# First mixer norm: squares summed along the token rows as loaded, factors spread by TensorE, no barrier, transposes at once

## The reference, cut to what matters

```
def rmsnorm(x, g):
    xf = x.astype(jnp.float32)
    y = xf * lax.rsqrt(jnp.mean(xf * xf, axis=-1, keepdims=True) + EPS)
    return (y * g.astype(jnp.float32)).astype(x.dtype)
...
xn = rmsnorm(x, norm_mix[l])
...
q, f, i, g = jnp.split(xn @ w_in, 4, axis=-1)
```

## Time and profile before

| | |
|---|---|
| median of 3 runs | 2931.27 us (2928.22 to 2931.78) |
| the profiled execution | 2926.66 us, of which the span of its instructions is 2924.9 us |
| mean granted TensorE clock | 0.978 of 2.4 GHz |
| busy share of the span | PE 95%, DVE 42%, ACT 20%, POOL 37% |
| chain of work that ended last | PE 87%, DVE 7%, ACT 2% |

### The profile page before, as it was taken

How to read it: one execution, slowest core, us unless ns; L and a number is a source line. 1 busy time by engine, 2 the same in 40 slices (tenths; PEclk the granted TensorE clock), 3 DMA queues, 4 the chain that set the end, 5 groups by cost and what they waited for, 6 DMA issues and landing times.

```text
span 2924.9 us, 43391 instructions
## 1 busy us (share of the span) xinstructions
PE 2790.2 (95%) x17613; PEld 2698.3 (92%) x17613; DVE 1240.5 (42%) x2145; ACT 580.5 (20%) x1158; POOL 1080.4 (37%) x938
## 2 busy tenths in 40 slices
PE   4999999989999999999999999976999999999998
PEld 3999999979999999999999887765799999999998
DVE  6244445443533333333361444556543333333335
ACT  4122222221300000000020233345030000000003
POOL 4333333313444334433346313311443443344331
PEclk7999999989999999999999999988999999999999
DMA  3111111131111111111122111145321111111211
GB/s 102 37 45 52 52 52 52 50 105 45 44 44 44 58 44 44 44 53 49 44 89 65 58 40 48 53 139 188 112 58 44 44 45 57 44 44 44 58 44 59
DMA packets 202239, 175.04 MB, mean 60 GB/s; under 512 B 6290, under 2 KB 185093, under 8 KB 202062
## 3 DMA queue, kind: packets, MB, share of 16 engines
q1 hardware_dynamic: 161728, 138.49, 15.3%
q10 hardware_dynamic: 40334, 33.95, 3.6%
HBM read 147.06 MB, written 25.36 MB: 59 GB/s over the span
## 4 chain that ended last, share of the span: by engine, by line
PE 87%; DVE 7%; ACT 2%; DMA 1%; POOL 1%; issue 1%; SPq 0%; ACTq 0%; PEld 0%; DVEq 0%; POOLq 0%; PEldq 0%
PE ps L709 25%; PE ps L711 25%; PE ps L710 25%; PE ps L904 3%; PE ps L1128 2%; PE ps L1148 1%; DMA k_page<-in_cache_k 1%; DVE rstd L1857 1%; DVE k_page L2196 1%; DVE stats L2130 1%; ACT probs L1621 1%; DVE act_lo L1862 1%; DVE act_whole L1814 1%; PE ps L1236 0%; PE ps L937 0%
## 5 line engine op out<-in xcount | busy, mean ns | idle before, releaser
L709 PE MATMUL ps<-act_hi,w_hi 128*128 128x344 f32 (+2 forms) x3808 | 1244.1, 327 | 30.2 <-DVE act_lo L1840 15.0
L711 PE MATMUL ps<-act_hi,w_lo 128*128 128x344 f32 (+2 forms) x3808 | 1221.4, 321 | 0.0
L710 PE MATMUL ps<-act_lo,w_hi 128*128 128x344 f32 (+2 forms) x3808 | 1221.4, 321 | 0.0
L668 POOL TENSOR_TENSOR w_hi<-w_stage,ones 128x512 fp32r<-128x512 f32 (+1 forms) x412 | 429.1, 1072 | 1382.8 <-PEq L759 1306.7
L709 PEld LDWEIGHTS ps<-act_hi,w_hi 128*128 128x128 f32 x3808 | 719.4, 189 | 46.9 <-issue 32.5
L710 PEld LDWEIGHTS ps<-act_lo,w_hi 128*128 128x128 f32 x3808 | 719.4, 189 | 3.8 <-issue 2.0
L711 PEld LDWEIGHTS ps<-act_hi,w_lo 128*128 128x128 f32 x3808 | 719.1, 189 | 0.0
L672 POOL TENSOR_TENSOR w_lo<-w_stage,w_hi 128x512 fp32r<-128x512 f32 (+1 forms) x412 | 540.0, 1342 | 8.1
L2044 DVE TENSOR_TENSOR resid<-resid,ps 128x344 f32<-128x344 f32 x528 | 269.9, 513 | 188.8 <-PE ps L711 188.5
L709 PE MATMUL ps<-h_hi,w_hi 128*128 128x344 f32 x1056 | 339.2, 321 | 2.6 <-DVE resid L2044 2.6
L710 PE MATMUL ps<-h_lo,w_hi 128*128 128x344 f32 x1056 | 337.1, 319 | 0.0
(11 more groups left out here) (279 smaller groups left out, 2225.3 us busy)
## 6 DMA issues: line engine op xcount, KB each, us to landing
w_stage<-in_w_gate_up SPq DMA_DIRECT2D x88, 512.0 KB, 4.9
w_stage<-in_w_down SPq DMA_DIRECT2D x44, 512.0 KB, 3.9
w_stage<-in_w_in_a SPq DMA_DIRECT2D x32, 512.0 KB, 5.2
w_stage<-in_w_kv SPq DMA_DIRECT2D x16, 512.0 KB, 4.3
k_page<-in_cache_k SPq DMA_DIRECT2D x16, 512.0 KB, 4.4
v_page<-in_cache_v SPq DMA_DIRECT2D x16, 512.0 KB, 6.3
w_stage<-in_w_out_b SPq DMA_DIRECT2D x12, 512.0 KB, 4.6
x_spill<-resid ACTq DMA_DIRECT2D x8, 516.0 KB, 2.9
```

The costliest lines, as they stand in the source:

```text
L668: last = g.tensor_tensor(hi[:, part], WST[:, part], ones[:, 0:1].to_broadcast([P, quarter]), ALU.mult)
L709: pe.matmul(out, wh, xh, start=first, stop=False)
L710: pe.matmul(out, wh, xl, start=False, stop=False)
L711: return pe.matmul(out, wl, xh, start=False, stop=last)
```

## The change

The factors no longer come from the transposed stream. ACT squares each block as it lies in `xs`, tokens on partitions, with an accumulated sum per row into a column of `frs` (`final_rstd`), then takes Ln and Exp of those 8 columns (and of one for the sample rows). DVE multiplies the identity by each column: eight 128x128 diagonal matrices and one of 8x8, in chunk 7 of `act_whole`. TensorE multiplies them by a matrix of ones, which spreads each token's factor over all partitions, into PSUM banks 6 and 7 (and 4 for the sample columns). DVE's product of X, gain and factor reads those banks in place of `rstd`, over 1024 columns; the 8 sample columns are done apart.

The transposes use three pairs of banks in turn and begin once the identity, the ones and the epsilon column stand (`consts` 1; the masks behind them raise it to 2, which PE, ACT and DVE wait for later). DVE alone copies a whole block of `X`. The barrier is gone. POOL's split of slab 1 waits until all 8 rests of the first norm are made, and ACT waits for the lower-bound vectors (`lb_ready`) ahead of its first evacuation. The small-vector work of DVE moves: its first part behind the copies of `X`, its second behind the last rest.

```diff
-        def phases_through(name):
-            return 3 * (PHASES.index(name) + 1)
-
-        def barrier(eng, name):
-
-            eng.drain().then_inc(phase_done, 1)
-            eng.wait_ge(phase_done, phases_through(name))
-
...
@@ GpSimd @@
+            g.memset(epst[:], EPS).then_inc(consts, 1)
             step(g.memset(pick[:], 0.0))
             step(g.memset(pick[:, 7:8], 1.0))
-            step(g.memset(epst[:], EPS))
...
+                if n == 1:
+                    pool.wait_ge(operand_split, C)
...
@@ TensorE @@
-            def norm(ph, squares):
-
-                pe.wait_ge(norm_acc, (nth(ph) + 1) * (C - 1))
-                for t in range(NT):
-                    last = pe.matmul(PS[:, t, 0:TS], ones[:], squares[:, 0, tile(t)], start=True, stop=True)
-                last.then_inc(norm_ss_full, 1)
-
...
             pe.wait_ge(consts, 1)
+            for b in range(NB):
+                pe.wait_ge(chunk_in[b], 16)
+                if b > 2:
+                    pe.wait_ge(io_copied[0], b - 2)
+                for c in range(C):
+                    last = pe.transpose(PS[:, 2 * (b % 3) + c // 4, c % 4 * P:(c % 4 + 1) * P], xs[:, b, c * P:(c + 1) * P], ident[:])
+                last.then_inc(io_full[0], 1)
             pe.wait_ge(vec_in, 16 * 11)
             pe.transpose(PS[:, 7, 0:78], RS[0:78, 0:P], ident[0:78, 0:78]).then_inc(vec_full, 1)
+            pe.wait_ge(xs_in, 16)
+            pe.wait_ge(io_copied[0], 6)
+            for c in range(C):
+                last = pe.transpose(PS[:, 4, c * DEC:(c + 1) * DEC], xss[:, c * P:(c + 1) * P], ident[0:DEC, 0:DEC])
+            last.then_inc(io_full[0], 1)
+            pe.wait_ge(vec_ready, 1)
+            pe.matmul(PS[:, 5, 0:2], ones[:], lam[:, 6:8], start=True, stop=True).then_inc(lam_full, 1)
             for b in range(NB):
-                pe.wait_ge(chunk_in[b], 16)
-                for u in range(2):
-                    q = 2 * b + u
-                    if b:
-                        pe.wait_ge(io_copied[u], b)
-                    for c in range(4):
-                        last = pe.transpose(PS[:, q % 2, c * P:(c + 1) * P], xs[:, b, (4 * u + c) * P:(4 * u + c + 1) * P], ident[:])
-                    last.then_inc(io_full[u], 1)
-            pe.wait_ge(xs_in, 16)
-            pe.wait_ge(io_copied[0], NB)
-            for c in range(C):
-                last = pe.transpose(PS[:, 0, c * DEC:(c + 1) * DEC], xss[:, c * P:(c + 1) * P], ident[0:DEC, 0:DEC])
-            last.then_inc(io_full[0], 1)
-
-            pe.wait_ge(vec_ready, 1)
-            pe.matmul(PS[:, 6, 0:2], ones[:], lam[:, 6:8], start=True, stop=True).then_inc(lam_full, 1)
-            barrier(pe, "loaded")
-            norm("mix0", XL32)
+                pe.wait_ge(x_diag, b + 1)
+                pe.matmul(PS[:, 6 + b // 4, b % 4 * P:(b % 4 + 1) * P], ones[:], XL32[:, C - 1, b * P:(b + 1) * P],
+                          start=True, stop=True)
+            pe.wait_ge(x_diag, NB + 1)
+            pe.matmul(PS[:, 4, 0:DEC], ones[0:DEC, :], XL32[0:DEC, C - 1, SEQ:T], start=True, stop=True).then_inc(norm_ss_full, 1)
+            pe.wait_ge(consts, 2)
...
@@ ScalarE @@
-            def square_block(b):
-
-                act.wait_ge(io_copied[0], b + 1 + (b == NB - 1))
-                act.wait_ge(io_copied[1], b + 1)
-                a.activation(XH32[:, :, block_span(b)], X[:, :, block_span(b)], ACT.Square).then_inc(norm_sq, 1)
-
+            act.wait_ge(consts, 1)
+            a.activation(lnt[:], epst[:], ACT.Ln)
             for b in range(NB):
-                act.wait_ge(io_full[0], b + 1)
-                a.copy(X[:, 0:4, b * P:(b + 1) * P], PS[:, 0, :].rearrange("p (c n) -> p c n", c=4)).then_inc(io_copied[0], 1)
-                if b:
-                    square_block(b - 1)
-            act.wait_ge(io_full[0], NB + 1)
-            a.copy(X[:, :, SEQ:T], PS[:, 0, 0:64].rearrange("p (c n) -> p c n", c=C)).then_inc(io_copied[0], 1)
-            square_block(NB - 1)
+                act.wait_ge(chunk_in[b], 16)
+                a.activation(XH32[:, b, 0:SEQ], xs[:, b, :], ACT.Square, accum_out=frs[:, b:b + 1]).then_inc(x_squared, 1)
+            act.wait_ge(xs_in, 16)
+            a.activation(XL32[0:DEC, 0, 0:SEQ], xss[:], ACT.Square, accum_out=frs[0:DEC, NB:NB + 1]).then_inc(x_squared, 1)
+            act.wait_ge(x_squared, NB + 1)
+            a.activation(frs[:, 0:NB], frs[:, 0:NB], ACT.Ln, bias=epst[:], scale=1.0 / D)
+            a.activation(frs[0:DEC, NB:NB + 1], frs[0:DEC, NB:NB + 1], ACT.Ln, bias=epst[0:DEC, :], scale=1.0 / D).then_inc(x_squared, 1)
+            act.wait_ge(x_squared, NB + 2)
+            a.activation(frs[:, 0:NB], frs[:, 0:NB], ACT.Exp, scale=-0.5)
+            a.activation(frs[0:DEC, NB:NB + 1], frs[0:DEC, NB:NB + 1], ACT.Exp, scale=-0.5).then_inc(x_squared, 1)
...
-            a.activation(lam[:, 0:2], PS[:, 6, 0:2], ACT.Exp).then_inc(vec_exp, 1)
-            barrier(act, "loaded")
-
-            def norm(ph):
-
-                a.activation(lnt[:], epst[:], ACT.Ln)
-                act.wait_ge(norm_ss_full, OLD.index(ph) + 1)
-                rs3 = RS[:].rearrange("p (t n) -> p t n", t=NT)
-                a.activation(rs3, PS[:, 0:NT, 0:TS], ACT.Ln, bias=epst[:], scale=1.0 / D).then_inc(norm_ln, 1)
-                act.wait_ge(norm_ln, OLD.index(ph) + 1)
-                a.activation(RS[:], RS[:], ACT.Exp, scale=-0.5).then_inc(norm_rs, 1)
+            a.activation(lam[:, 0:2], PS[:, 5, 0:2], ACT.Exp).then_inc(vec_exp, 1)
...
-            norm("mix0")
-
             split_hi("mix0")
+            act.wait_ge(consts, 2)
+            act.wait_ge(lb_ready, 1)
...
@@ VectorE @@
+            for b in range(NB):
+                dve.wait_ge(io_full[0], b + 1)
+                pair = 2 * (b % 3)
+                v.tensor_copy(X[:, :, b * P:(b + 1) * P],
+                              PS[:, pair:pair + 2, :].rearrange("p u (c n) -> p (u c) n", n=P)).then_inc(io_copied[0], 1)
...
-            def sum_block(b):
-
-                dve.wait_ge(norm_sq, b + 1)
-                ins = v.tensor_reduce(XL32[:, 0, block_span(b)], XH32[:, :, block_span(b)].rearrange("p c n -> p n c"), AX, ALU.add)
-                if b:
-                    ins.then_inc(norm_acc, 1)
-
+            dve.wait_ge(io_full[0], NB + 1)
+            v.tensor_copy(X[:, :, SEQ:T], PS[:, 4, 0:64].rearrange("p (c n) -> p c n", c=C)).then_inc(io_copied[0], 1)
+
+            dve.wait_ge(x_squared, NB + 3)
             for b in range(NB):
-                dve.wait_ge(io_full[1], b + 1)
-                v.tensor_copy(X[:, 4:8, b * P:(b + 1) * P], PS[:, 1, :].rearrange("p (c n) -> p c n", c=4)).then_inc(io_copied[1], 1)
-                if b > 1:
-                    sum_block(b - 2)
-            sum_block(NB - 2)
-            sum_block(NB - 1)
+                v.tensor_scalar(XL32[:, C - 1, b * P:(b + 1) * P], ident[:], frs[:, b:b + 1], None, ALU.mult).then_inc(x_diag, 1)
+            v.tensor_scalar(XL32[0:DEC, C - 1, SEQ:T], ident[0:DEC, 0:DEC], frs[0:DEC, NB:NB + 1], None, ALU.mult).then_inc(x_diag, 1)
+            dve.wait_ge(io_copied[0], NB + 1)
+            dve.wait_ge(norm_ss_full, 1)
+            step(v.tensor_tensor(XL32[:, :, SEQ:T], X[:, :, SEQ:T], vec(G_MIX0).unsqueeze(2).to_broadcast([P, C, DEC]), ALU.mult))
+            step(v.tensor_tensor(XL32[:, :, SEQ:T], XL32[:, :, SEQ:T], PS[:, 4, 0:DEC].unsqueeze(1).to_broadcast([P, C, DEC]),
+                                 ALU.mult))
+            factor = PS[:, 6:8, :].rearrange("p u n -> p (u n)")
+
+            def mix_rest(c):
+
+                dve.wait_ge(hi_ready, c + 1)
+                v.tensor_tensor(XL[:, c, :], XL32[:, c, :], XH[:, c, :], ALU.subtract).then_inc(operand_split, 1)
+
+            for c in range(C):
+                v.scalar_tensor_tensor(out=XL32[:, c, 0:SEQ], in0=factor, scalar=vec(G_MIX0)[:, c:c + 1], in1=X[:, c, 0:SEQ],
+                                       op0=ALU.mult, op1=ALU.mult).then_inc(whole_ready, 1)
+                if c:
+                    mix_rest(c - 1)
+            mix_rest(C - 1)
             dve.wait_ge(vec_exp, 1)
             step(v.tensor_tensor(tmp8[:, 8:16], tmp8[:, 0:8], tmp8[:, 16:24], ALU.add))
             step(v.reciprocal(tmp8[:, 8:16], tmp8[:, 8:16]))
             step(v.tensor_tensor(lbv[:], tmp8[:, 0:8], tmp8[:, 8:16], ALU.mult))
-            step(v.tensor_scalar(oml[:], lbv[:], -1.0, 1.0, ALU.mult, ALU.add))
+            v.tensor_scalar(oml[:], lbv[:], -1.0, 1.0, ALU.mult, ALU.add).then_inc(lb_ready, 1)
             dve.wait_ge(vec_exp, 2)
             step(v.tensor_tensor(lam[:, 2:3], lam[:, 0:1], lam[:, 1:2], ALU.subtract))
-
             step(v.tensor_scalar(lam[:, 3:4], lam[:, 2:3], -1.0, -LAM_INIT, ALU.mult, ALU.add))
-            barrier(dve, "loaded")
-
-            def scale_split(ph, gain, split=True):
-
-                def rest(c):
-                    dve.wait_ge(hi_ready, hi_before(ph) + c + 1)
```

(20 more changed lines are left out.)

16 lines of the change are left out of this document (5 added, 11 removed).

## The result

The changed kernel takes 2910.16 us (median of 4 runs, 2907.25 to 2915.39) against 2930.38 us for the kernel before on the same chip (4 runs, 2928.22 to 2931.78): a ratio of 0.9936, 95% interval 0.9924 to 0.9948. That is 20.2 us less (the interval is 15.2 to 22.3), where 18.35 were summed and a time of 2913 was forecast. Run again later with five runs of its own, it took 2912.79 against 2929.05: 16.3 us less, a ratio of 0.9950 (0.9936 to 0.9963).

A forecast was written before the change was run, and what follows sets the result against it. An opening limited by VectorE and one serial passage precedes a program limited by TensorE. The group after chunk 7 moves from 73.05 to 53.7 us, 19.35 won, less 1 for the clock: 18.35, so 2913 us, range 2904 to 2919.

The forecast's parts named there:

- Factors at 21.0, copies by 21.2: Opening: ScalarE's factors stand at 21.0 us; VectorE's copies and first small-vector work end at most at 21.2.
- Diagonals held, products at 30.1: VectorE's diagonals each wait behind one POOL instruction of slab 0's split, ending at 29.2; wide products start at 30.1 us.
- the rival of diagonals not held: Diagonals run free of POOL: products start at 25.0, last rest ends near 44.8, 2908.4 us in all; chance 0.17.
- Sixteen operations of 1.2, last rest at 49.3: VectorE's eight products and eight rests, without POOL, take 19.2 us; last rest ends at 49.3 instead of 71.26.
- Lower bounds 2.5, load 1.30, first evacuation 0.47, group at 53.7: After the last rest: lower-bound work, Silu's table load and first evacuation delay TensorE's next group to 53.7 us.
- a race for the start: Lower-bound operations and POOL's slab 1 split, released together, compete; the first one or two operations should win.
- more held work: Lower bounds end 3.6 us behind the last rest, plus 2 us more of half clock: 2916 us; chance 0.15.
- the load's drain: Silu's table load on ScalarE also costs a drain, as the skill page says: 1.4 us later, 2914.3; chance 0.05.
- The clock: 1 us: TensorE's clock falls for part of the group after its pause of some 2.9 us, costing 1 us.
- Half clock through head 0: TensorE stays at half clock, up to 2947 us; chance 0.03 for 3.5 to 6.7 groups, 0.03 for more.
- Slab 1 late: POOL's split, started at 49.3, is ready at 65.9 when TensorE wants it at 65.1: 2913.7 us; chance 0.05.
- The sum: TensorE's group after chunk 7 starts 19.35 us earlier, less 1 for the clock: 18.35 us won.

The follow-up runs named there:

- after_again: The changed kernel itself, nothing altered, run again in a later set beside the kernel before: 2912.79 us, ratio 0.9950 (0.9936 to 0.9963).

## Why the prediction was right, step by step

- **Factors at 21.0, copies by 21.2.** Factors at 20.36, the last small copy at 19.48: 0.6 and 1.7 early. None of the small work was held, because the last of it began before GpSimd did at 19.36. Neither error reaches the products, since GpSimd's end sets their start.
- **Diagonals held, products at 30.1.** Right: 30.54, and 29.48 in after_again. GpSimd's end, 28.46 where 28.5 was predicted, set it. Two kernels that free the diagonals show it from both sides, and the rival of diagonals not held falls. That the number came so near is in part luck. Seven GpSimd instructions held a diagonal each, and not six, so the nine ended at 28.67 and not at 29.2. The end of the spreading and the two sample products then took 1.87 and not 0.9, with TensorE at half clock (0.50 from 28.6 to 30.5). The two errors cancel in part. (The 1.16 of the earlier trace rows is a mean as well: one of its four took 0.66 and the others 1.38 to 1.44.)
- **Sixteen operations of 1.2, last rest at 49.3.** Right: 49.41. But the reason given, that slab 1 waits, is only part of it: without that wait the sixteen took 21.17 us in place of 18.87, against 26.42 in the old kernel, since products that read PSUM leave GpSimd its turn. At head 1 the wait alone is worth 7.3 us in the old kernel, the rest of the change alone 19.4 (111.03 - 91.64), both 18.0, with 1.4 lost to the clock there: the two gains are largely the same one.
- **Lower bounds 2.5, load 1.30, first evacuation 0.47, group at 53.7.** Right: two operations held, in all six executions in which the last rest releases slab 1 ahead of them; 2.14, 1.29, 0.61, and 53.52. But a race for the start, which the prediction gave as the reason, does not show. In all six the first operation began ahead of GpSimd; the second, the reciprocal, began 0.02 to 0.04 us behind GpSimd's start and still took 0.20, and no run shows why. The rivals of more held work and of the load's drain fall. TensorE's pause ahead of that group was 2.19 us and not 2.9, since chunk 7 ended 1.92 behind the last rest and not 1.45. The earlier trace rows already showed 1.79 for it (71.26 to 73.05), for TensorE is still at chunk 6 when the last rest ends.
- **The clock: 1 us.** It took 1.4 us (40.09 against 38.66), and 1.4 to 1.5 in five of six executions with that pause. Half clock through head 0 was not seen: the clock was 1.00 from 56.7 to 90 us.
- **Slab 1 late.** It was not: TensorE is busy for all of 55 to 90 us, with GpSimd's split done at 58.60.
- **The sum.** 18.35 predicted, 18.03 at head 1's first evacuation, 20.2 and 16.3 in the two pairs of medians. The one is about as far above as the other is below, so that the medians bear out the sum to some 2 us and no closer.

What stays open: what makes the clock fall in five executions of six and not in the sixth, and which of the later stages the 7 us between executions belong to one by one. Splitting slab 0 late together with the early load was not tried.

## What to carry to other kernels

Before pricing a small operation, look at what GpSimd runs at that moment: here eight operations that take 1.66 us alone took 8.19, and with their source in PSUM 2.14. Two remedies for the same contention do not add; ask of each what it is worth when the other is there. Where executions differ by several us in stages that the change doesn't touch, read a change in the opening from the first event behind it that all kernels share, and use the medians of one set for the rest.
